# Second layer of a two-layer decoder trunk: all eight conditioning pieces of the mixer's pause run in that pause, and six tiles of squares are summed in four column groups

## What is computed

```python
def modulate(y, i):
    return rms_norm(y, g_pre[i]) * (1.0 + mod[:, i, 1]) + mod[:, i, 0]

def residual(y, out, i, w):
    return y + w * mod[:, i, 2] * rms_norm(out, g_post[i])

mod = (jax.nn.silu(c) @ a_w + a_b).reshape(B, N_SUB, 3, D_MODEL)[:, :, :, None, :]
```

## Time and profile before

| | us |
|---|---|
| median of 3 runs | 1373.47 |
| lowest and highest | 1371.69, 1375.74 |
| the profiled execution's own time | 1373.03 |
| its span in the trace | 1371.2 |
| TensorE busy | 1333.3 (97%) |
| VectorE busy | 683.8 (50%) |
| ScalarE busy | 538.7 (39%) |
| granted TensorE clock, mean of the run | 0.995 of full speed |

### The profile page before, as it was taken

How to read it: one execution, slowest core, us unless ns; L and a number is a source line. 1 busy time by engine, 2 the same in 40 slices (tenths; PEclk the granted TensorE clock), 3 DMA queues, 4 the chain that set the end, 5 groups by cost and what they waited for, 6 DMA issues and landing times.

```text
span 1371.2 us, 23285 instructions
## 1 busy us (share of the span) xinstructions
PE 1333.3 (97%) x10150; PEld 1236.8 (90%) x10150; DVE 683.8 (50%) x735; ACT 538.7 (39%) x641; POOL 85.0 (6%) x103
## 2 busy tenths in 40 slices
PE   5999999999989999999999999999999999999997
PEld 3899999979969799999979999998898779999996
DVE  3434434367875644434463444434778664444443
ACT  4433233343445533333343233333443554333331
POOL 0000000000270000000000000000017100000000
PEclk9999999999999999999999999999999999999998
DMA  9965566365325644446375544656541473443531
GB/s 370 353 250 185 192 230 228 148 236 210 123 95 225 227 157 149 153 176 255 122 276 193 180 149 154 227 202 216 200 154 65 149 273 124 147 149 138 198 135 39
DMA packets 50372, 255.43 MB, mean 186 GB/s; under 512 B 7022, under 2 KB 12014, under 8 KB 30062
## 3 DMA queue, kind: packets, MB, share of 16 engines
q1 hardware_dynamic: 50110, 253.08, 50.8%
q0 software_dynamic: 176, 1.09, 0.2%
HBM read 249.26 MB, written 4.89 MB: 185 GB/s over the span
## 4 chain that ended last, share of the span: by engine, by line
PE 93%; DVE 2%; DMA 2%; ACT 1%; issue 1%; SPq 0%; DVEq 0%; ACTq 0%
PE PS L506 28%; PE PS L508 27%; PE PS L507 27%; PE PS L518 3%; PE PS L570 1%; DMA z<-in_ada 1%; PE PS L707 1%; DMA stage<-in_ada_w 1%; PE PS L726 1%; PE PS L749 0%; PE PS L927 0%; DVE raw L1647 0%; PE PS L672 0%; PE PS L578 0%; PE PS L854 0%
## 5 line engine op out<-in xcount | busy, mean ns | idle before, releaser
L506 PE MATMUL PS<-hmh,WHI 128*128 128x320 f32 x1856 | 576.8, 311 | 3.9 <-DVE hml L1350 3.4
L508 PE MATMUL PS<-hmh,WLO 128*128 128x320 f32 x1856 | 571.3, 308 | 0.0
L507 PE MATMUL PS<-hml,WHI 128*128 128x320 f32 x1856 | 571.3, 308 | 0.0
L1307 DVE TENSOR_TENSOR WLO<-raw,WHI 128x2048 fp32r<-128x2048 f32 (+1 forms) x148 | 365.5, 2470 | 406.6 <-ACT WHI L1015 406.6
L1015 ACT ACTIVATE WHI<-raw 128x2048 fp32r<-128x2048 f32 (+1 forms) x148 | 304.0, 2054 | 354.8 <-PE PS L508 349.6
L506 PEld LDWEIGHTS PS<-hmh,WHI 128*128 128x128 f32 x1856 | 348.2, 188 | 25.6 <-issue 23.5
L507 PEld LDWEIGHTS PS<-hml,WHI 128*128 128x128 f32 x1856 | 348.3, 188 | 0.3
L508 PEld LDWEIGHTS PS<-hmh,WLO 128*128 128x128 f32 x1856 | 348.1, 188 | 0.0
L506 PE MATMUL PS<-hhl,WHI 128*128 128x320 f32 x704 | 216.6, 308 | 0.0
L507 PE MATMUL PS<-hhl,WHI 128*128 128x320 f32 x704 | 216.5, 308 | 0.0
L508 PE MATMUL PS<-hhl,WLO 128*128 128x320 f32 x704 | 216.5, 308 | 0.0
(11 more groups left out here) (249 smaller groups left out, 819.5 us busy)
## 6 DMA issues: line engine op xcount, KB each, us to landing
raw<-in_w_in SPq DMA_DIRECT2D x88, 1024.0 KB, 4.8
raw<-in_w_out SPq DMA_DIRECT2D x32, 1408.0 KB, 5.9
stage<-in_ada_w SPq DMA_DIRECT2D x82, 512.0 KB, 7.7
ada<-in_ada_w SPq DMA_DIRECT2D x46, 512.0 KB, 5.4
raw<-in_m_in SPq DMA_DIRECT2D x20, 1024.0 KB, 4.8
raw<-in_m_out SPq DMA_DIRECT2D x8, 1024.0 KB, 4.8
z<-in_ada SPq DMA_DIRECT2D x3, 1024.0 KB, 13.1
big<-in_ada SPq DMA_DIRECT2D x2, 1024.0 KB, 19.5
```

The costliest lines, as they stand in the source:

```text
L506: mm(out, hi, rhi, start=first, stop=False)
L507: mm(out, hi, rlo, start=False, stop=False)
L508: return mm(out, lo, rhi, start=False, stop=last)
L1307: tt(WLO[:, slot, 0:width], raw[:, slot, 0:width], WHI[:, slot, 0:width].bitcast(F32), ALU.subtract).then_inc(s_lo[slot], 1)
```

## The change

Pieces 56 to 58 leave the second layer's mixer (`AT_TAIL` keeps the first layer alone). Pause 4 now takes the eight pieces 56 to 63, all of them ahead of the sums of the squares of x (`FRONT[4]` is 8). Their homes are those of `OUT_GAP`: P0, P1, P2, P3, ada, S0, S1 and P0 again. SyncE issues the first five where it issued five before, and the last three at the start of the next block, behind the wait for the output projection and behind the stores.

The sums in pause 4 are made by `packed_stats`. The squares of tiles 0 to 5 are multiplied by ones 32 columns wide, in column groups 0, 1, 2, 3, 0, 1, into bank 4, so that each group of 32 partitions holds a part of the sum. ScalarE copies this bank to `rt` with a factor of 1/32 before it squares the last tile, and a full product of ones with `rt` adds it to the sums of tiles 6 and 7 in bank 5.

Everything else keeps its order. The constants `BEHIND` become `COUNT` and `FRONT`; for pauses 0 to 3 they give the same five and three as before.

```diff
-HOMES = FIRST_HOMES + FFN_GAP + IN_TAIL + OUT_GAP + FFN_GAP + ["ada"] * 5 + FFN_GAP + IN_TAIL + OUT_GAP[:5]
-AT_GAP, AT_TAIL, AT_OUT, AT_FFN = {0: 16, 2: 35, 3: 48}, (24, 56), (27, 59), {3: 43}
-BEHIND = {0: 3, 1: 3, 2: 3, 3: 3, 4: 0}
+HOMES = FIRST_HOMES + FFN_GAP + IN_TAIL + OUT_GAP + FFN_GAP + ["ada"] * 5 + FFN_GAP + OUT_GAP
+AT_GAP, AT_TAIL, AT_OUT, AT_FFN = {0: 16, 2: 35, 3: 48}, {0: 24}, (27, 56), {3: 43}
+COUNT = {0: 8, 1: 8, 2: 8, 3: 8, 4: 8}
+FRONT = {0: 5, 1: 5, 2: 5, 3: 5, 4: 8}
+PACKED = (4,)
...
                         sp.wait_ge(s_used[1], l * ITS + OFF_MO + IT_MO + 1)
-                        for p in range(AT_OUT[l] + 5, AT_OUT[l] + 5 + BEHIND[n - 1]):
+                        for p in range(AT_OUT[l] + 5, AT_OUT[l] + COUNT[n - 1]):
                             piece(p)
...
-                    if it == 1:
+                    if it == 1 and l in AT_TAIL:
                         piece(AT_TAIL[l])
...
-                sp.wait_ge(ev["gr"], 6 * l + 5)
-                piece(AT_TAIL[l] + 1)
-                sp.wait_ge(ev["sc0"], l + 1)
-                piece(AT_TAIL[l] + 2)
+                if l in AT_TAIL:
+                    sp.wait_ge(ev["gr"], 6 * l + 5)
+                    piece(AT_TAIL[l] + 1)
+                    sp.wait_ge(ev["sc0"], l + 1)
+                    piece(AT_TAIL[l] + 2)
                 out_weights(1)
...
+            def packed_stats(n):
+
+                for k in range(6):
+                    j = k % 4
+                    pe.wait_ge(s_sqx, KT * n + k + 1)
+                    last = mm(PS[32 * j:32 * j + 32, 4, 0:T], ones[:, 0:32], sq[:, k, :], start=(k < 4), stop=(k > 1))
+                last.then_inc(s_xg, 1)
+                pe.wait_ge(s_sqx, KT * n + 7)
+                mm(PS[:, 5, 0:T], ones, sq[:, 6, :], start=True, stop=False)
+                pe.wait_ge(s_xc, PACKED.index(n - 1) + 1)
+                mm(PS[:, 5, 0:T], ones, rt[:], start=False, stop=False)
+                pe.wait_ge(s_sqx, KT * n + 8)
+                mm(PS[:, 5, 0:T], ones, sq[:, 7, :], start=False, stop=True).then_inc(s_xst, 1)
...
                 if p is not None:
-                    for i in range(5):
+                    for i in range(FRONT[n]):
                         partial(p + i)
-                if n < 3 * DEPTH - 1:
+                if n in PACKED:
+                    packed_stats(n + 1)
+                elif n < 3 * DEPTH - 1:
                     x_stats(n + 1)
                 if n in WHOLE:
                     turned(WHOLE[n])
                 for _ in range(KEPT_BUSY.get(n, 0)):
                     mm(PS[:, 4, 0:T], ones, cst[:, 0:T], start=True, stop=True)
                 if p is not None:
-                    for i in range(5, 5 + BEHIND[n]):
+                    for i in range(FRONT[n], COUNT[n]):
                         partial(p + i)
...
                 for a, b in SUMS:
+                    if b == KT and n - 1 in PACKED:
+                        act.wait_ge(s_xg, PACKED.index(n - 1) + 1)
+                        a_(rt[:], PS[:, 4, 0:T], ACT.Copy, scale=1 / 32).then_inc(s_xc, 1)
                     act.wait_ge(s_x, KT * n + b)
                     a_(sq[:, a:b, :], x[:, a:b, :], ACT.Square).then_inc(s_sqx, b - a)
...
-                act.wait_ge(s_part, AT_TAIL[l] + 4)
+                if l in AT_TAIL:
+                    act.wait_ge(s_part, AT_TAIL[l] + 4)
...
-                x_norm(3 * l + 2, 1, AT_OUT[l] + 6 if l == 0 else None)
+                x_norm(3 * l + 2, 1, AT_OUT[l] + 6)
```

More of the change, by code:

```diff
@@ L294, in trunk @@
         s_xst = sem("s_xst")
+        s_xg = sem("s_xg")
+        s_xc = sem("s_xc")
         s_r = sem("s_r")
@@ L409, in ffn_in @@
                         sp.wait_ge(s_used[1], l * ITS + OFF_MO + IT_MO + 1)
-                        for p in range(AT_OUT[l] + 5, AT_OUT[l] + 5 + BEHIND[n - 1]):
+                        for p in range(AT_OUT[l] + 5, AT_OUT[l] + COUNT[n - 1]):
                             piece(p)
                     if n == 3:
-                        free_ffn((l - 1) * ITS + OFF_F1O + IT_OUT - 1, AT_GAP[2])
+                        free_ffn((l - 1) * ITS + OFF_F1O + IT_OUT - 1, 2)
                     ahead = 5 if n in AT_FFN else 0
@@ L420, in ffn_in, with free_ffn @@
                         both(it)
-            def free_ffn(last, p0):
+            def free_ffn(last, n):
+                p0 = AT_GAP[n]
                 sp.wait_ge(s_used[0], last + 2)
@@ L427, in free_ffn @@
                 sp.wait_ge(s_used[1], last + 2)
-                for p in range(p0 + 6, p0 + 8):
+                for p in range(p0 + 6, p0 + COUNT[n]):
                     piece(p)
@@ L446, in _ @@
                     if it == 0:
-                        free_ffn(l * ITS + OFF_F0O + IT_OUT - 1, AT_GAP[3 * l])
-                        sp.wait_ge(s_part, AT_GAP[3 * l] + 9)
+                        free_ffn(l * ITS + OFF_F0O + IT_OUT - 1, 3 * l)
+                        sp.wait_ge(s_part, AT_GAP[3 * l] + COUNT[3 * l] + 1)
                         sp.dma_start(kc[:, :, 0:WIN], A["k"][l]).then_inc(s_cache, 16)
@@ L799, in mixer @@
                 last.then_inc(ev["dsm"], 1)
-                partial(AT_TAIL[l])
+                if l in AT_TAIL:
+                    partial(AT_TAIL[l])
                 pe.wait_ge(ev["un"], 6 * (l + 1))
@@ L822, in mixer @@
                                       eb[rows, col:col + TS], start=True, stop=True)
-                    if a == 0:
+                    if a == 0 and l in AT_TAIL:
                         partial(AT_TAIL[l] + 1)
@@ L835, in mixer @@
                 last.then_inc(ev["pt"], 1)
-                partial(AT_TAIL[l] + 2)
+                if l in AT_TAIL:
+                    partial(AT_TAIL[l] + 2)
                 def blocks(n, bank):
```

## The result

| | median of the runs (us) | runs | ratio to before, 95% |
|---|---|---|---|
| before | 1375.68 | 6 | |
| changed | 1386.76 | 6 | 1.0089 [1.0067, 1.0110] |
| changed, measured again later | 1389.99 | 6 | 1.0097 [1.0070, 1.0125] |

The change costs 0.9 to 1.0%, some 12 to 13 us, where 8.8 were forecast. The sign was right. The first median is at the upper end of the range (1387), and the second, 1389.99, is above it. The profiled execution of the changed kernel took 1386.27 us (span 1384.5), 13.2 us more than the one of before.

What follows compares the result with a forecast made beforehand. TensorE was taken to bound the kernel (93% of the chain of waits). Landings +9.3, sums -1.9, clock +2.4 and mixer -1.0 gave +8.8 us on 1373.03, so 1381.8 us (chance 0.52), range 1376.5 to 1387.

Steps and rivals of the forecast that it cites:

- The sign: Whole run: the changed kernel would be slower, by over 0.3% with chance 0.88.
- The landings: Pause 4: TensorE waits for pieces 61 to 63, landing as in pause 1, so the sums start 9.3 us later.
- The packed sums: Pause 4, sums to root: 3.0 us against 4.9, as most squares are done beforehand; -1.9 us.
- The clock in the pause: Pause 4: clock halves during the waits and returns during the sums or transposes; +2.4 us, bounds 0 and about +7.
- Rival 1: Pause 4: the clock holds, so the pause costs +7.4 and the whole +6.4, 1379.4 us; chance 0.20.
- rival 2: Pause 4: the clock stays low into the entry, +5 to +7 in place of +2.4, 1385.5 us; chance 0.13.
- The mixer: Second layer's mixer: removing piece 56 gives 0, 57 gives -1.0, 58 gives 0; -1.0 us, bounds 0 and -2.0.
- The execution it was summed on: Whole run: terms were added to the profiled execution's 1373.03 us, taken as 0.4 us under the median.

Runs made afterwards that it cites:

- f1_all_three_filled: Changed kernel with useless products of constants (one piece's shape) at the places pieces 56, 57 and 58 left in the second layer's mixer; 1389.54 us, ratio 1.0091.
- f5_pause_filled: `f1_all_three_filled` plus 4, 2 and 2 full products of constants ahead of pieces 61, 62 and 63 in pause 4; 1383.94 us, ratio 1.0053.
- e1_mixer_filled: Changed kernel with four useless products of constants where piece 56 stood in the second layer's mixer; 1388.35 us, ratio 1.0093.
- e4_no_loads: `e1_mixer_filled` with pieces 61 to 63 not loaded but multiplied from already full buffers (wrong weights); 1380.95 us, ratio 1.0039.
- e3_packed_only: Kernel before with `packed_stats` in pause 4 and nothing else changed; 1377.13 us, ratio 1.0014.
- g1_mixer_pieces_skipped: Kernel before with pieces 56 to 58 still loaded, but only one product of 8 columns done for each in the mixer; 1379.54 us, ratio 1.0025.
- g2_all_filled_no_loads: `f1_all_three_filled` with pieces 61 to 63 not loaded, as in `e4_no_loads`; 1377.14 us, ratio 1.0012.
- f3_before_filled: Kernel before with useless products near the start, at each mixer's start and ahead of line 810; 1379.15 us, ratio 1.0028.
- f2_pieces_before_stores: Changed kernel with pieces 61 to 63 issued ahead of the second layer's stores instead of behind them; 1388.68 us, ratio 1.0113.
- e2_piece56_later: Kernel before with piece 56 multiplied behind the products of line 810 instead of ahead of them; 1380.9 us, ratio 1.0032.
- g3_pause1_before_stores: Kernel before with pieces 32 to 34 issued ahead of the first layer's stores, in pause 1; 1374.78 us, ratio 0.9989.

## Why the prediction was right or wrong

The forecast was +8.8 us; measured are +12.9 in the means. By its steps:

- **The landings: right.** Forecast for piece 63: 14.1 us after the pause's start. It was 14.1 in the changed kernel, 14.0 in its second trace, 13.4 in `f1_all_three_filled`, 13.0 in `f5_pause_filled` and 12.9 in `e1_mixer_filled`. Pause 1 was a good twin, and `e4_no_loads` shows that the landing is the cause.
- **The packed sums: right, and for the reason given.** 3.2 us for 3.0 forecast. The six tiles took 1.25 us of records for 1.1. The forecast rested on squares that are done when the sums begin, and `e3_packed_only` shows that without this nothing is saved (5.2 us for 4.9). The pause at full clock (`f5_pause_filled`) came to +6.3 for +7.4 forecast, since the last landing was 1.1 us earlier in that trace.
- **The clock in the pause: it fell and came back as forecast, at half to all of the size.** +2.4 was forecast. On the path from piece 63 to the root the traces of the changed kernel, of `f1_all_three_filled` and of the changed kernel again have 1.2, 1.7 and 2.3 us more than `f5_pause_filled`, and the clock came back before the entry: root to first `hml` is unchanged. Rival 1, that it holds, and rival 2, that it stays low, did not happen in the traces.
- **The mixer: wrong. This is the step that failed.** It said of piece 56: "Taking the piece away makes TensorE wait longer for the same VectorE instruction: 0"; of 57 -1.0, and of 58 0, in all -1.0 with bounds 0 and -2.0. For the work on the path that is right: the rest of `g1_mixer_pieces_skipped` is -0.7. What the step left out is that the pieces were what kept TensorE's clock up between products that are small and wait for others. Without them the time at half the clock grows by 10.7 us, worth 4.0, so the mixer costs about +3 and does not give 1 (`g1_mixer_pieces_skipped`: +3.2 in the mean). I had priced the clock in the pause, where TensorE would stand, and not in the mixer, where I had just written that TensorE would stand longer.
- **The execution it was summed on.** The sum went against an execution at clock 0.995, while the average run of before has 0.992. That hid how often time is lost to the clock even with the pieces in place, and it put the forecast's time too low by itself: 1373.03 was taken as 0.4 us under the median, and with six runs the median is 1375.68.
- **The range: held by luck.** Its upper part was there for rival 2, which did not happen; that 1386.76 is so far up comes from the mixer's clock and the low start of the sum.

By terms: the landing at 14.1 us and the 4.05 us behind it at full clock make 18.15 from the pause's start to the root, +7.4 (forecast +7.4); mixer work -0.7 (-1.0); clock in the mixer +4.0 (not priced); clock in the pause +2.5, 6.8 us at 0.37 (+2.4). That is 13.2 for 12.9 measured.

The theory behind the four fills, that work in the waits holds the clock, is shown over the runs by `g1_mixer_pieces_skipped` and by the pair `e4_no_loads` and `g2_all_filled_no_loads`; `f5_pause_filled` agrees. Its rival, that a fall comes by chance, is right about the single run: the first layer's mixer, whose code is the same in all kernels but `f3_before_filled`, lost the clock in the traces of `e1_mixer_filled`, `e3_packed_only`, `e4_no_loads` and others, and kept it in that of before and in the first of the changed kernel. How often and for how long it falls is what the change moved.

The traces have the same order, with a limit. The second layer's mixer stood at half the clock for 17, 14, 10 and 14 us where the three pieces' work was gone (the changed kernel twice, `f2_pieces_before_stores`, `g1_mixer_pieces_skipped`), and for 7 us in each of the three kernels with all places filled. Where the pieces stood it did not fall in four of five traces (not in before, `e2_piece56_later`, `e3_packed_only` and `g3_pause1_before_stores`; 10 us in `f3_before_filled`). So the fillers shortened the fall and did not shut it out, and they do not stand for the pieces in every way; why is open.

## What to carry to other kernels

A small piece of work that fills a wait of TensorE has two values: its own time, and the clock it keeps up for what follows. When such a piece is moved away, price the half clock at the place it leaves as well as at the place it goes to, most of all where the products behind it are small and wait for other engines. Where a load's buffer comes free only at a block's end, count its landing before its product is put ahead of work on which the next block waits: here that cost 7.4 us at full clock, with 1.7 us saved in the sums already in it. The form of pause 1, with the last three pieces behind the sums, was not tried in pause 4. And where time follows the clock from run to run, compare kernels at the same granted clock, over ten runs or so, before a difference of 0.3% is believed.

## What the runs showed that I had not expected

- **The clock can fall at a short stop.** In the changed kernel TensorE stood 1.7 us and the clock went from 1.00 to 0.50, and stayed there for 17 us in which it was hardly ever idle: the stretch 1066 to 1070 is busy for 4.00 us of 4 and stands at 0.50. The busy time of small products (64x8, 128x64) does not show whether the clock will come back. In its second trace, in `g1_mixer_pieces_skipped` and in `f2_pieces_before_stores` the stop at this place was 1.5 to 2.0 us, and the clock fell 0.7 to 2.7 us behind it. The length of one stop does not settle it: behind 1.67 us in pause 1 of `g3_pause1_before_stores` the clock held, and in the mixer of `e4_no_loads` it fell 2.2 us behind a stop of 0.53. The Trainium skill ("TensorE: Matmul & The Clock Gate", section "Why this matters for your kernels") speaks of gaps between bursts of matmuls that have to be kept short. By the gap that it names a stop as short as this one would have left the clock up, and the mixer's term would have been the forecast's; the traces differ, and decide.
- **The same program is 1372 to 1385 us by its clock alone.** The 71 runs of before show 0.37 us for each us at half the clock, and two traces of the changed kernel have the falls in different places. The same page of the Trainium skill (section "What's actually happening") says that the gate's observation runs free of the kernel, which would make it so; the runs agree in that the place varies with nothing in the program changed.
- **Added work can make a kernel faster**: eight products in the mixer 3.9 us (`g2_all_filled_no_loads` against `e4_no_loads`, standard error 1.7), eight in the pause 4.9 us (`f5_pause_filled` against `f1_all_three_filled`, 1.5), each of them with about 12 us less at half the clock. None of these kernels beat the one before.
- **Six DMAs of 3.1 MB took 11.9 us** from the first issue (1119.04) to the last piece's products (1130.92), with 430 GB/s only in the stretch from 1128. The fit of the Trainium skill's page "DMA: Bandwidth & Descriptors" (section "Anatomy of one DMA"), 2 us and then 436 GB/s for one DMA of another issuing path, would give as an estimate 9.2 us; the measured time decides, and the forecast had rightly gone by pause 1.
